# Two transformer-like blocks on one core: fewer divided matmuls, and one buffer 128 bytes further on

## The chip, the cores and the metric

One core of one Trainium2 chip runs the whole program. The metric is the device time of one execution in microseconds (us); the median over several executions is given.

## The reference

256 tokens of width 2048 go through two blocks, in float32. Cut to what matters:

```
first block:   z = rms(x) @ w_in;  differential attention and a gated spatial mix
               h = x + mixed @ w_out
               f = rms(h);  h += (silu(f @ w1) * (f @ w3)) @ w2        # hidden width 5632
               h += (p @ pl_w_up) * sigmoid(h @ pl_w_gate)             # p: per-layer input, width 256
second block:  16 meta tokens ahead of the 256
               u, gb, gc, v, ga, gbr = split(rms(h) @ w_in_2)
               y_a = pool(u) @ pool_w;  y_b = (gb * conv(gc * v)) @ conv_out_w
               h += (sigmoid(ga) * y_a + sigmoid(gbr) * y_b) @ w_o
               h += (silu(gate) * up) @ w_down                         # hidden width 5632
               out = rms(h)
```

## The kernel before, in words

Nearly all of the time is matrix products. Each weight matrix is cut into **pieces** of 256 rows by 512 columns; there are 940. SyncE's queue loads two pieces at a time (1 MB) into `raw`, a ring of four. ScalarE writes a piece's rounded high part into `hi` (L487), VectorE the rest, raw minus high, into `lo` (L814); `hi` and `lo` are rings of four pieces. The activations are held in two parts in the same way, in the buffers `A`, `B` and, for the per-layer input, `PT`.

The products are listed in order by `schedule()` as **segments**: v, qk, g, u, out, f1_up0, f1_down0, f1_up1, f1_down1, f1_up2, f1_down2, plup, plgate, ga, u2, pool, conv, gbr, cout, wo, f2_up0, f2_down0, f2_up1, f2_down1, f2_up2, f2_down2. A segment has turns, a turn has groups (two for most), and a group has pieces (8 for most, 6 in f1_down2 and f2_down2, 2 in pool, 1 in plup). A group makes 512 output columns in four banks of PSUM; its index in the turn is `g`, the piece's index in the group `j`. In the two-pass layouts a piece gives TensorE 24 matmuls of 128x128 weights by 256 columns: `highs` (L1362) makes 16, for each of two `kk` the high part of the weights with both parts of the activations (`part`), over four `m`; `lows` (L1373) makes 8, the low part of the weights with the high part of the activations. One segment follows another without a pause; the semaphores are waited for, but they are set in time.

Other forms: u2 has 272 columns and conv's first two kinds 258 columns (L1409 to L1411); v, g and the f2_down segments have 512 columns, with the activations as the stationary side (L1391 to L1393).

`turns_of` runs a segment's turns: a segment of one turn, and on TensorE the first `peel` turns of the others, are written out with `t` = 0, 1, ...; the rest is a hardware loop, in which `t` is None. f1_up0, f2_up0, out, ga and conv have `peel=1`; plup, pool and u2 have one turn; plgate, f2_up1, f2_up2, f1_down0, f1_up1 and others have `peel=0`.

`SIDE` puts small work between pieces of the first turn: in f1_up0 after piece 6 `first_ffn_rstd` (four matmuls with `ones`), in f2_up0 transposes of `h` after pieces 3 and 11 and `ffn_rstd` after piece 6, in ga `double_rstd` after piece 6.

**Divided matmuls.** In the segments that `TWO_STEPS` names, `highs` divides one matmul of the first piece (`j == 0`) of every group, the fifth of the piece, into two over neighbouring columns with the same weights: L1359 takes columns 0 to `at_col`, L1360 the rest.

**Where the buffers lie.** The tensors stand behind one another in each partition, in the order of their declarations (starts rounded up to 32 bytes). `hi` and `lo` take 16384 bytes each. From the start of `hi`, `A` begins at 35008 bytes and `B_halves`, the part of `B` that most segments read, at 69312: both 192 past a multiple of 256. `PT` stands behind `silu_s` and `UP` in an overlay and begins at 159040 bytes from `hi`, 64 past a multiple of 256. All rows within `A`, `B` and `PT`, and all weight blocks, are multiples of 256 bytes apart.

Of the kernel before, what the change touches and what calls it, by code (L numbers as in the profile page):

```python
# [23 lines left out]
F32R = mybir.dt.float32r  # L24

P = 128
D = 2048
T = 256
META = 16
TM = META + T  # L30
KT = D // P
GC = 512
MT = GC // P
# [127 lines left out]
for _step, _at in (("norm_stats", 0), ("norm_root", 1), ("norm_scale", 2)):  # L161
# [1 line left out]
SIDE.setdefault(("u", 14), []).append("gate_mix0")  # L163

TWO_STEPS = {"f1_up0": 128, "f1_down0": 240, "f1_up1": 224, "f1_down1": 192, "f1_up2": 64, "f1_down2": 16, "plgate": 252,
             "f2_up1": 248, "f2_up2": 8}

class Tally:  # L170
# [38 lines left out]
def bass_two_blocks(nc, ins, out):  # L209
    SEGS, TOTAL = schedule()  # L210

    with ExitStack() as ctx:
# [6 lines left out]
        def overlay(**shapes):  # L219

            with ExitStack() as own:
                return [own.enter_context(nc.sbuf_tensor(n, s[0], s[1])) if isinstance(s, tuple) else
                        own.enter_context(nc.sbuf_tensor(n, s, F32)) for n, s in shapes.items()]
# [13 lines left out]
        line, _, = overlay(line=[P, LINE], pad_line=[P, 1])  # L237
        _, qk = overlay(pad_qk=[P, 8 * BROW], qk=[P, 16, T])
        _, xtok = overlay(pad_x=[P, 8 * BROW], xtok=[P, 2, D])
# [18 lines left out]
        _, relb_in, meta_in, vin1, vin2, relb, onehot, lamv, rb = overlay(  # L258
            v_skip=[P, 2048 - 8], relb_in=[32, HEADS], meta_in=[META, D], vin1=[V1N, P], vin2=[V2N, P], relb=[32, HEADS, 32],
            onehot=[32, LINE], lamv=[P, 4, P], rb=[P, 2, P])  # L260
        _, ws_in = overlay(ws_skip=[P, 2 * 1024 + 2048 + 2048 + 1024 + 1024 + 1024], ws_in=[P, 8, P])
        silu_s, UP, PT = overlay(silu_s=[P, MT, T], UP=[P, KT, T], PT=([P, 2, 2 * T], F32R))
        G1, G2 = overlay(G1=[P, KT, T], G2=[P, KT, T])
        _, win_a, win_b, win_c = overlay(g1_a=[P, KT * T], win_a=[P, MT, TM], win_b=[P, MT, TM], win_c=[P, MT, TM])
        _, cvv, cvg, cvo = overlay(g1_b=[P, KT * T], cvv=[P, MT, TV], cvg=[P, MT, TV], cvo=[P, MT, T])
        _, HT, gfin_row = overlay(silu_b=[P, MT * T], HT=[P, 2, D], gfin_row=[P, D])
        sb("arena", [P, 10368])

        ps = ctx.enter_context(nc.psum_tensor("ps", [P, 8, 512], F32))
# [1031 lines left out]
        def _(pe):  # L1301
            done, v_in, s_in = Tally(pe_done), Tally(v_to_pe), Tally(s_to_pe)

            def wait(tally):
                pe.wait_ge(tally.sem, tally.now())
# [26 lines left out]
            def high(slot, kk, m):  # L1332
                return hi[:, slot % RING, kk, m * P:(m + 1) * P]
# [4 lines left out]
            def activations(buf, layout):  # L1338
                return {"A": A, "B": {"halves": B_halves, "token": B_token}.get(layout, B), "PT": PT}[buf]

            def two_passes(seg, g):

                layout = seg.reads[1]
                return layout in ("halves", "wide_halves") or (layout == "conv" and seg.kinds[g] == "cb")

            def highs(seg, g, j, slot, b0, n):

                buf, layout, _ = seg.reads
                X = activations(buf, layout)
                at = 0 if layout == "halves" else META  # L1350
                pe.wait_ge(hi_ready, n + 1)
                for kk in range(2):
                    k = 2 * j + kk + (4 * WIDEST_FIRST[g] if seg.name == "pool" else 0)
                    for part in range(2):
                        x = X[:, k, at + part * T:at + (part + 1) * T]
                        for m in range(MT):
                            at_col = TWO_STEPS.get(seg.name, 0) if j == 0 and kk == 0 and part == 1 and m == 0 else 0
                            if at_col:
                                pe.matmul(ps[:, b0 + m, 0:at_col], high(slot, kk, m), x[:, 0:at_col], start=False, stop=False)  # L1359
                                pe.matmul(ps[:, b0 + m, at_col:T], high(slot, kk, m), x[:, at_col:T], start=False, stop=False)  # L1360
                            else:
                                pe.matmul(ps[:, b0 + m, 0:T], high(slot, kk, m), x, start=j == 0 and kk == 0 and part == 0, stop=False)  # L1362

            def lows(seg, g, j, slot, b0, n):

                buf, layout, _ = seg.reads
                X = activations(buf, layout)
                pe.wait_ge(lo_ready, n + 1)
                for kk in range(2):
                    k = 2 * j + kk + (4 * WIDEST_FIRST[g] if seg.name == "pool" else 0)  # L1370
                    Xh = X[:, k, 0:T] if layout == "halves" else X[:, k, META:TM]
                    for m in range(MT):
                        last = pe.matmul(ps[:, b0 + m, 0:T], low(slot, kk, m), Xh, start=False,  # L1373
                                         stop=j == seg.pieces - 1 and kk == 1)
                last.then_inc(pieces_used, 1)
# [156 lines left out]
            def last_pieces(seg, b0):  # L1532

                first = seg.pieces - RING
                for a in range(2):
                    for j in range(first, seg.pieces):
                        n = TOTAL - seg.pieces + j
                        if a == 0:
                            pe.wait_ge(lo_ready, n + 1)
                        for kk in range(2):  # L1540
                            k = 2 * j + kk
                            Xh, Xl = B_token[:, k, a * P:(a + 1) * P], B_token[:, k, T + a * P:T + (a + 1) * P]
                            to = ps[:, b0 + a, :]
                            pe.matmul(to, Xh, hi[:, n % RING, kk, :], start=False, stop=False)  # L1544
                            pe.matmul(to, Xh, lo[:, n % RING, kk, :], start=False, stop=False)  # L1545
                            last = pe.matmul(to, Xl, hi[:, n % RING, kk, :], start=False, stop=j == seg.pieces - 1 and kk == 1)  # L1546
                        if a == 1:
                            last.then_inc(pieces_used, 1)
                    if a == 0:
                        last.then_inc(half_done, 1)  # L1550

            for seg in SEGS:
                def run(turn, t):
                    for g, kind in enumerate(seg.kinds):
                        G = turn * len(seg.kinds) + seg.g0 + g
                        b0 = 4 * ((seg.g0 + g + (t or 0) * len(seg.kinds)) % 2)
                        if seg.name == "v" and g == 1:
                            pe.wait_ge(x_kept, 2)
                        elif not isinstance(G, int) or G >= 2:
                            pe.wait_ge(psum_free, G - 1)  # L1560
                        if t == 0 and g == 0 and seg.name == "qk":
                            wait(v_in)
                            wait(s_in)
                        at_end = isinstance(G, int) and G == SEGS[-1].g0 + MT - 1
                        for j in range(seg.pieces - RING if at_end else seg.pieces):
                            n = turn * seg.per_turn + seg.p0 + g * seg.pieces + j
                            slot = seg.p0 + g * seg.pieces + j + (t or 0) * seg.per_turn
                            chunk = g if seg.name == "pool" else j // 2
                            if seg.name == "pool" and j == 0 or seg.name not in ("pool", "plup") and g == 0 and j % 2 == 0:
                                pe.wait_ge(act_ready, seg.reads[2] + chunk + 1)  # L1570
                            beside = SIDE.get((seg.name, g * seg.pieces + j), ()) if t == 0 else ()
                            if not two_passes(seg, g):
                                piece(seg, g, j, slot, b0, n)
                            else:
                                highs(seg, g, j, slot, b0, n)
                                lows(seg, g, j, slot, b0, n)
                            for what in beside:
                                side(seg, what, G)
                        if at_end:
                            last_pieces(seg, b0)  # L1580
                turns_of(pe, seg, {}, run)
# [33 lines left out]
```

## Time and profile before

| | |
|---|---|
| median of 3 runs | 2645.22 us (2645.04 to 2645.64) |
| profiled execution | 2644.93 us |
| its span, first to last instruction | 2643.1 us |
| mean granted TensorE clock | 0.999 |
| TensorE matmuls | 21427, 100% of the span busy |
| VectorE busy | 1571.9 us, 59% |
| ScalarE busy | 1172.6 us, 44% |

The profile gives each instruction of one execution its start, its duration and what released it. Matmuls overlap one another, so their durations (276 ns and more) say less than the distances between their starts. In the chain of waits a row's second number is the time up to the next link, and with equal matmuls it is that distance times their count.

### The profile page before, as it was taken

The numbers are of one execution on the slowest core, as the hardware profiler recorded it, in microseconds if no ns is written. First come the engines' busy times: TensorE is split into PE (matmuls) and PEld (weight loads), VectorE is DVE, ScalarE is ACT, GpSimd is POOL, SyncE is SP. The second block draws the span as 40 slices with busy tenths as digits, with TensorE's granted clock in tenths as the row PEclk, the third lists the DMA queues.
The fourth block names the chain that finished last, engine by engine and source line by source line (L and its number), as shares of the span: only waits on it lengthen the run. The fifth ranks groups of instructions, "written<-read, shape, count | busy, mean of one in ns | idle before, by whom it ended". The sixth has DMA issues, their size and how long they took to land.

```text
span 2643.1 us, 50947 instructions
## 1 busy us (share of the span) xinstructions
PE 2630.4 (100%) x21427; PEld 2568.2 (97%) x21427; DVE 1571.9 (59%) x1557; ACT 1172.6 (44%) x1259; POOL 0.8 (0%) x7
## 2 busy tenths in 40 slices
PE   9999999999999999999999999999999999999998
PEld 7989999999999999999999999999999989998997
DVE  6567765555555556795666666556755555554555
ACT  5446544434443444454433333444554434443444
POOL 0000000000000000000000000000000000000000
PEclk9999999999999999999999999999999999999999
DMA  8644655555655565555555555655555555555553
GB/s 295 197 162 148 204 192 191 191 192 190 194 188 199 189 199 192 177 203 194 176 176 190 179 189 178 201 189 198 191 194 195 199 192 191 190 191 191 190 191 128
DMA packets 254275, 503.33 MB, mean 190 GB/s; under 512 B 8130, under 2 KB 11652, under 8 KB 253988
## 3 DMA queue, kind: packets, MB, share of 16 engines
q1 hardware_dynamic: 252180, 497.61, 56.8%
q10 hardware_dynamic: 1952, 3.68, 0.4%
q8 instruction: 106, 1.74, 0.3%
q14 instruction: 37, 0.30, 0.0%
HBM read 498.37 MB, written 2.88 MB: 190 GB/s over the span
## 4 chain that ended last, share of the span: by engine, by line
PE 99%; DMA 0%; DVE 0%; ACT 0%; SPq 0%; issue 0%; DVEq 0%; ACTq 0%
PE ps L1362 49%; PE ps L1373 24%; PE ps L1391 4%; PE ps L1393 4%; PE ps L1392 4%; PE ps L1409 4%; PE ps L1410 4%; PE ps L1411 4%; PE ps L1401 0%; PE ps L1402 0%; PE ps L1403 0%; DMA xtok<-in_x_dram 0%; PE ps L1360 0%; PE ps L1546 0%; PE ps L1545 0%; PE ps L1544 0%
## 5 line engine op out<-in xcount | busy, mean ns | idle before, releaser
L814 DVE TENSOR_TENSOR lo<-raw,hi 128x1024 fp32r<-128x1024 f32 x940 | 1144.2, 1224 | 931.3 <-ACT hi L487 916.8
L487 ACT ACTIVATE hi<-raw 128x1024 fp32r<-128x1024 f32 x940 | 991.3, 1060 | 1255.8 <-PE ps L1373 945.9
L1362 PE MATMUL ps<-A,hi 128*128 128x256 f32 x7256 | 909.1, 277 | 0.0
L1362 PEld LDWEIGHTS ps<-A,hi 128*128 128x128 f32 x7256 | 863.3, 188 | 0.3
L1362 PE MATMUL ps<-B,hi 128*128 128x256 f32 x3956 | 491.6, 276 | 0.0
L1373 PE MATMUL ps<-A,lo 128*128 128x256 f32 x3648 | 489.3, 277 | 0.0
L1362 PEld LDWEIGHTS ps<-B,hi 128*128 128x128 f32 x3956 | 468.0, 188 | 0.1
L1373 PEld LDWEIGHTS ps<-A,lo 128*128 128x128 f32 x3648 | 448.8, 188 | 0.0
L1373 PE MATMUL ps<-B,lo 128*128 128x256 f32 x1984 | 265.2, 276 | 0.0
L1373 PEld LDWEIGHTS ps<-B,lo 128*128 128x128 f32 x1984 | 243.3, 188 | 0.0
L1410 PE MATMUL ps<-B,hi 128*128 128x258 f32 (+1 forms) x768 | 219.7, 286 | 0.0
L1411 PE MATMUL ps<-B,lo 128*128 128x258 f32 (+1 forms) x768 | 219.5, 286 | 0.0
L1409 PE MATMUL ps<-B,hi 128*128 128x258 f32 (+1 forms) x768 | 219.4, 286 | 0.0
L1409 PEld LDWEIGHTS ps<-B,hi 128*128 128x128 f32 x768 | 145.9, 190 | 0.0
L1411 PEld LDWEIGHTS ps<-B,lo 128*128 128x128 f32 x768 | 145.4, 189 | 0.0
L1410 PEld LDWEIGHTS ps<-B,hi 128*128 128x128 f32 x768 | 144.2, 188 | 0.0
L1392 PE MATMUL ps<-lo,B 128*128 128x512 f32 x336 | 130.7, 389 | 0.0
L1393 PE MATMUL ps<-hi,B 128*128 128x512 f32 x336 | 130.7, 389 | 0.0
L1391 PE MATMUL ps<-hi,B 128*128 128x512 f32 x336 | 130.7, 389 | 0.0
L1393 PEld LDWEIGHTS ps<-hi,B 128*128 128x128 f32 x336 | 63.1, 188 | 13.1
L1391 PEld LDWEIGHTS ps<-hi,B 128*128 128x128 f32 x336 | 63.1, 188 | 13.0
L1392 PEld LDWEIGHTS ps<-lo,B 128*128 128x128 f32 x336 | 63.1, 188 | 13.0
(247 smaller groups left out, 1226.7 us busy)
## 6 DMA issues: line engine op xcount, KB each, us to landing
raw<-in_w_in_dram SPq DMA_DIRECT2D x136, 1024.0 KB, 5.1
raw<-in_ffn_w_dram SPq DMA_DIRECT2D x132, 1024.0 KB, 5.1
raw<-in_w_gate_up_dram SPq DMA_DIRECT2D x88, 1024.0 KB, 5.0
raw<-in_w_down_dram SPq DMA_DIRECT2D x44, 1024.0 KB, 5.0
raw<-in_w_out_dram SPq DMA_DIRECT2D x16, 1024.0 KB, 4.9
raw<-in_pl_w_gate_dram SPq DMA_DIRECT2D x16, 1024.0 KB, 5.0
raw<-in_conv_out_w_dram SPq DMA_DIRECT2D x16, 1024.0 KB, 5.0
raw<-in_w_o_dram SPq DMA_DIRECT2D x16, 1024.0 KB, 5.0
```

The lines of the kernel that those rows point to most:

```text
L487: act.activation(hi[:, slot % RING], raw[:, raw_slot, 2 * (slot % 2):2 * (slot % 2) + 2, :], ACT.Copy).then_inc(hi_ready, 1)
L814: dve.tensor_tensor(lo[:, slot % RING], raw[:, slot // 2 % RAWS, 2 * (slot % 2):2 * (slot % 2) + 2, :], hi[:, slot % RING], ALU.subtract). ...
L1362: pe.matmul(ps[:, b0 + m, 0:T], high(slot, kk, m), x, start=j == 0 and kk == 0 and part == 0, stop=False)
L1373: last = pe.matmul(ps[:, b0 + m, 0:T], low(slot, kk, m), Xh, start=False, stop=j == seg.pieces - 1 and kk == 1)
L1391: pe.matmul(to, Xh, hi[:, slot % RING, kk, :], start=first, stop=False)
L1392: pe.matmul(to, Xh, lo[:, slot % RING, kk, :], start=False, stop=False)
L1393: last = pe.matmul(to, Xl, hi[:, slot % RING, kk, :], start=False, stop=final)
L1409: pe.matmul(to, Wh, Xh, start=first, stop=False, skip_group_check=True)
L1410: pe.matmul(to_low, Wh, Xl, start=False, stop=False, skip_group_check=True)
L1411: last = pe.matmul(to, Wl, Xh, start=False, stop=final, skip_group_check=True)
```

## The change

`TWO_STEPS`, with a column for each of nine segments and every group, gives way to one column, 248, and a list of places. A place is a segment's name with the index of a piece in the turn (`g * seg.pieces + j`). In the turn with `t == 0` the list `IN_STEPS` holds, in every other turn the shorter list `IN_STEPS_EVER`. The divided matmul is still the fifth of its piece. The products are the same. `PT` gets 32 float32 words (128 bytes) ahead of it in its overlay.

```diff
-TWO_STEPS = {"f1_up0": 128, "f1_down0": 240, "f1_up1": 224, "f1_down1": 192, "f1_up2": 64, "f1_down2": 16, "plgate": 252,
-             "f2_up1": 248, "f2_up2": 8}
+STEP = 248
+IN_STEPS_EVER = {("f2_up1", 0), ("f2_up2", 0)}
+IN_STEPS = IN_STEPS_EVER | {("f1_up0", 8), ("plup", 0), ("plgate", 0), ("pool", 0), ("f2_up0", 8), ("f2_up0", 12)}
...
-        silu_s, UP, PT = overlay(silu_s=[P, MT, T], UP=[P, KT, T], PT=([P, 2, 2 * T], F32R))
+        silu_s, UP, _, PT = overlay(silu_s=[P, MT, T], UP=[P, KT, T], pad_pt=[P, 32], PT=([P, 2, 2 * T], F32R))
...
-            def highs(seg, g, j, slot, b0, n):
+            def highs(seg, g, j, slot, b0, n, in_steps):
...
-                            at_col = TWO_STEPS.get(seg.name, 0) if j == 0 and kk == 0 and part == 1 and m == 0 else 0
-                            if at_col:
-                                pe.matmul(ps[:, b0 + m, 0:at_col], high(slot, kk, m), x[:, 0:at_col], start=False, stop=False)
-                                pe.matmul(ps[:, b0 + m, at_col:T], high(slot, kk, m), x[:, at_col:T], start=False, stop=False)
+                            if in_steps and kk == 0 and part == 1 and m == 0:
+                                for a, b in ((0, STEP), (STEP, T)):
+                                    pe.matmul(ps[:, b0 + m, a:b], high(slot, kk, m), x[:, a:b], start=False, stop=False)
...
-                                highs(seg, g, j, slot, b0, n)
+                                highs(seg, g, j, slot, b0, n, (seg.name, g * seg.pieces + j) in (IN_STEPS if t == 0 else IN_STEPS_EVER))
```

## Rows read from the trace of the kernel before

**Rows 1.** The page: span, TensorE's granted clock in 40 slices, the last chain.
```profile
span 2643.1 us, 50947 instructions
...
PEclk9999999999999999999999999999999999999999
...
PE 99%; DMA 0%; DVE 0%; ACT 0%; SPq 0%; issue 0%; DVEq 0%; ACTq 0%
```

**Rows 2.** The page's groups: the work on each piece beside TensorE's.
```profile
L814 DVE TENSOR_TENSOR lo<-raw,hi 128x1024 fp32r<-128x1024 f32 x940 | 1144.2, 1224 | 931.3 <-ACT hi L487 916.8
L487 ACT ACTIVATE hi<-raw 128x1024 fp32r<-128x1024 f32 x940 | 991.3, 1060 | 1255.8 <-PE ps L1373 945.9
```

**Rows 3.** Line L1359, the first part of every divided matmul.
```profile
L1359 PE MATMUL ps<-A,hi x40: 168/242/277, 343.9 to 2547.4; 128*128 128x128 f32 x8, 128*128 128x224 f32 x8, 128*128 128x248 f32 x8, 128*128 128x64 f32 x6
...
L1359 PE MATMUL ps<-B,hi x12: 172/248/269, 519.8 to 1050.5; 128*128 128x240 f32 x4, 128*128 128x192 f32 x4, 128*128 128x16 f32 x4
```

**Rows 4.** Chain of waits (start, us, what): gbr's first piece, f2_up0's first.
```profile
1646.33 1.81 PE ps L1362 x16
...
1907.45 1.81 PE ps L1362 x16
```

**Rows 5.** Chain: divided matmuls of f1_up0 (turns 1 to 3), f1_up1, f1_down2: first and last.
```profile
388.63 0.06 PE ps L1359
...
498.06 0.06 PE ps L1359
...
607.44 0.10 PE ps L1359
...
760.55 0.10 PE ps L1359
...
1001.29 0.01 PE ps L1359
...
1050.62 0.01 PE ps L1359
```

**Rows 6.** Chain: end of f1_down2, plup's first piece, plgate's first matmuls.
```profile
1065.69 0.91 PE ps L1373 x8
1066.60 1.88 PE ps L1362 x16
...
1077.91 0.46 PE ps L1362 x4
```

**Rows 7.** Chain: pool's first matmuls, and conv's first.
```profile
1350.60 1.89 PE ps L1362 x16
...
1373.21 0.12 PE ps L1409
```

**Rows 8.** Chain: f1_up0, the piece behind `first_ffn_rstd`, and piece 8's second part.
```profile
363.45 1.89 PE ps L1362 x16
...
368.23 0.91 PE ps L1373 x8
```

**Rows 9.** Chain: f2_up0 from `ffn_rstd` on, the transposes, piece 12.
```profile
1928.69 1.88 PE ps L1362 x16
...
1942.83 1.75 PE ps L1495 x16
1944.58 1.83 PE ps L1362 x16
1946.41 0.91 PE ps L1373 x8
```

**Rows 10.** Chain: f2_up1's first piece, divided into 248 and 8.
```profile
2173.09 0.47 PE ps L1362 x4
...
2175.05 0.91 PE ps L1373 x8
```

**Rows 11.** Chain: f2_up2, its first three groups' divided pieces, and its end.
```profile
2435.17 0.47 PE ps L1362 x4
...
2457.89 0.47 PE ps L1362 x4
...
2459.85 0.91 PE ps L1373 x8
...
2481.77 0.94 PE ps L1373 x8
...
2568.89 0.94 PE ps L1373 x8
2569.83 0.23 PE ps L1391
```

## The prediction

> **What bounds the kernel now.** I read the page first: the chain that ended last is 99% TensorE, at a granted clock of nine tenths or more in every slice, which with the mean of 0.999 given in the table is the 2.4 GHz level throughout [rows 1]. So whatever changes TensorE's own stream changes the time one for one. VectorE and ScalarE need 1.22 and 1.06 us for each piece of weights [rows 2]; a piece takes TensorE 2.72 us [rows 4], and the waits of both engines before these instructions are long and end mostly on each other or on TensorE. A stream faster by some thousandths does not run into them, nor into the transfers of 1 MB for two pieces.
>
> Next I read the chain of waits piece by piece. A piece of 24 matmuls of 256 columns (16 with `hi`, 8 with `lo`) has one of two cadences. The reader should compare the durations of the "x16" and "x8" rows: 1.81 and 0.91 us, or 1.88 and 0.94.
> - **Plain:** gbr, cout and wo, 96 pieces or 2304 matmuls with no split and no interruption, take 1907.45 - 1646.33 = 261.12 us, 113.33 ns each [rows 4]. The three segments run in loops, and cross from B to A, to B and to A.
> - **Stretched:** pool takes (1373.21 - 1350.60) / 192 = 117.8 ns each [rows 7]; plup, (1077.91 - 1066.60) / 96 = 117.8 [rows 6]. It is 4.43 ns more for each matmul, at the same clock. Once there, f2_up2 stays there until something interrupts the run of equal matmuls [rows 11].
>
> **What a split costs in the plain cadence.** The 24 matmuls take 25 starts. From one divided matmul to the next lie 192 plain intervals (21.76 us) and what the split adds: with 128 and 128 columns (498.06 - 388.63) / 5 = 21.89 us, so 0.13; with 224 and 32 (760.55 - 607.44) / 7 = 21.87, so 0.11; with 16 and 240, over 144 intervals (16.32), (1050.62 - 1001.29) / 3 = 16.44, so 0.12 [rows 5]. That is 0.11 to 0.13 us a split, about one whole matmul interval, however few columns the smaller part has. I take 0.13 where the smaller part has 64 columns or more, 0.12 in f1_down2 and 0.11 elsewhere; the range over all 41 removed here is 4.5 to 5.3 us. 
>
> **The change, part by part.**
> 1. *Splits removed in plain stretches.* Before there are 40 + 12 = 52 [rows 3]. After, by the code: `t == 0` exists for the engine only where a segment has one turn or a first turn peeled off. f1_up0 keeps one (its piece 8), f2_up1 four and f2_up2 three, one a turn; plup, pool get one, f2_up0 two. plgate has two turns and nothing peeled on TensorE, so its `t` is None and its entry does nothing. That makes 12. Removed outside f2_up2: f1_up0 7 x 0.13, f1_down0 4 x 0.11, f1_up1 8 x 0.11, f1_down1 4 x 0.13, f1_up2 6 x 0.13, f1_down2 4 x 0.12, plgate 4 x 0.11, f2_up1 4 x 0.11 = 4.89 us. None of it lies beside other work on TensorE's path. That the plain cadence needs no upkeep is what rows 4 show; without that the price is that of rival 1.
> 2. *f2_up2.* It takes 2569.83 - 2435.17 = 134.66 us [rows 11], against 1152 x 113.33 = 130.56: 4.10 over. Its turns begin stretched, or are put there: the 8 and 248 split leaves one group stretched (2435.17 to 2457.89), the next plain (2459.85), the third stretched again (2481.77). f2_up1 is entered from the same kind of 512-column matmuls, also stretched (0.47 for four), and its 248 and 8 split brings it to plain at 2175.05 [rows 10], for 1.96 - 1.81 = 0.15 us. f2_up2 is now split in that way. New excess: 0.15 + 2 x 0.11 = 0.37. Gain 3.73 us. Bounds: 4.10 at most; if the split failed, all 1152 stretched (5.10) and three splits, a loss of 1.3.
> 3. *pool.* Now 192 x 4.43 ns = 0.85 over. With the split at the same place as in f2_up1 it should cost 0.15: gain 0.70. Bounds: -0.11 to 0.74.
> 4. *f2_up0.* After the norm's matmuls five pieces are stretched, 1928.69 to 1942.83 [rows 9]. The split in piece 8 leaves 28 stretched matmuls and ends the other 92 early: 92 x 4.43 = 0.41, less 0.13 for the split made in a stretched stream (0.15 less four stretched matmuls). The transposes after piece 11 restore the plain cadence already before the change (0.91 at 1946.41), so the split of piece 12 buys nothing and costs 0.11. Gain 0.17; bounds -0.24 to 0.30.
> 5. *f1_up0's piece 8* stays split, 248 and 8 instead of 128 and 128. It is entered stretched and must be left plain, as it is now [rows 8]. I count 0 for the other size, with 0.02 either way.
> 6. *PT 128 bytes on.* Entering plup the cadence changes with the first matmul that reads PT, and after it recovers within four matmuls on A (0.46 at 1077.91, before the next split) [rows 6]. By the declared sizes A and B_halves begin 192 bytes past a multiple of 256 from `hi`, PT 64; moved by 128, PT is as they are. I expect plain: 0.43 saved, 0.11 for the new split, 0.32 net. Bounds -0.11 to 0.32. No wait is added anywhere, no DMA or queue is touched, and UP and PT still fit into the arena.
>
> Sum: 4.89 + 3.73 + 0.70 + 0.17 + 0.32 = 9.81 us off the profiled execution's 2644.93 (span 2643.1 and 1.8 around it): 2635.1. The median of the runs is 0.3 above that execution, so 2635.4.
>
> **Rivals.**
> 1. *The stretched cadence is not left in f1_up0* (slower). What ends it there now is a split of 128 and 128; 248 and 8 has one witness from a stretched stream [rows 10], none in this place, and the same two parts in the other order fail in one entry and work in another [rows 11]. Nothing behind it interrupts the stream up to plup: 256 pieces, 6144 matmuls x 4.43 = 27.2 us. With plup's split as rescue: 2635.4 + 27.2 = 2662.6; without, 1032 more up to ga's norm, 2667. If the change from A to B at f1_down0 healed it (PT to A healed plup's), 56 pieces, 6.0 us: 2641.4. It decides from 9.81 / 0.00443 = 2200 matmuls, 92 pieces. For it: no safeguard is left. Against: 248 and 8 left a stretched stream plain, and 128 and 128 did here. 0.16, of which healed 0.03. A plain stream that falls stretched unaided in the same region would cost the same kind of sum; rows 4 speak against it.
> 2. *f2_up2's first split fails:* 1.3 lost instead of 3.73 won, 2640.5. Against it stands the like entry of f2_up1. 0.05.
> 3. *The small places fail* (pool, f2_up0, one or both): 0.8 + 0.4 at most, 2636.6. 0.08.
> 4. *The address does nothing:* plup stays at 117.8 and pays for a split: 0.32 + 0.11, 2635.9. That would be so if TensorE's reads met no obstacle that depends on the place; against it, both changes of cadence in rows 6 come with the buffer. 0.07. The Trainium skill (SBUF — State Buffer, Who interferes with whom) gives PE two independent read ports and says that it never waits on anyone, which is this rival; rows 6 do not agree with it easily.
>
> **How the numbers follow.** The summed forecast has 0.64. Within 2634.5 (all splits at 0.13) and 2641 lie forecast, rivals 2, 3 and 4: 0.84. A no-change reading is 0.2%, 5.3 us, either way. Faster: 0.64 + 0.08 + 0.07 = 0.79. Same: rival 2 and the healed part of rival 1, 0.08. Slower: 0.13.
>
> **What the profile after would show.** 12 split pairs; "x16" rows of 1.81 us from f1_up0's piece 9 on through f1_down2, without a break; PT rows of 1.81; in pool 1.88 for nothing past its first few matmuls; f2_up2 about 130.9 us long; f2_up0's pieces 9 to 11 at 1.81. If 1.88 stands behind 366 us, rival 1 is true and the prediction wrong; rows of 1.88 only from 2435 us on mean rival 2.

## The result, and the profile after

2668.52 us, median of four executions (2668.50 to 2668.55), against 2645.22: ratio 1.0088, 95% interval 1.007 to 1.0105. 23.3 us slower, where 9.8 us faster was forecast. The profiled execution took 2668.52 us with a span of 2666.7.

The page of the changed kernel: the span, the granted clock in 40 slices, the last chain. Only the span differs in a way that matters.

```profile
span 2666.7 us, 50867 instructions
...
PEclk9999999999999999999999999999999999999999
...
PE 99%; DVE 1%; ACT 0%; DMA 0%; issue 0%; DVEq 0%; ACTq 0%
```

TensorE is still the whole chain, at the full 2.4 GHz level (nine tenths or more in every slice; the mean granted clock is 0.999). The loss is a cadence, that is, the time from one matmul's start to the next one's, and the chain of waits of the changed kernel shows it (start, us, what; a divided matmul is now one row, L1360 x2). First f1_up0 from the norm's matmuls on, then plup's first piece and the last two pieces before ga's norm.

```profile
363.67 1.89 PE ps L1362 x16
...
366.50 0.47 PE ps L1362 x4
366.97 0.12 PE ps L1360 x2
...
368.49 0.94 PE ps L1373 x8
369.43 1.89 PE ps L1362 x16
...
1090.70 0.12 PE ps L1360 x2
...
1092.22 0.94 PE ps L1373 x8
...
1210.94 0.94 PE ps L1373 x8
1211.89 0.86 PE ps L1487 x4
...
1214.58 0.91 PE ps L1373 x8
```

The reader should follow the "x8" rows. Before, the piece behind the division had 0.91 [rows 8]; now it has 0.94, and so has every one up to ga's norm: 1211.89 - 366.50 = 845.39 us for 299 pieces, 7176 matmuls, 117.8 ns each. The division did not end the stretched cadence in f1_up0, and the one in plup did not either. ga's norm ended it.

Two other places failed too. In the chain, pool's first piece and f2_up0's piece 8 keep 0.94 behind their divisions (first two rows), whereas f2_up2's first piece goes to 0.91 (fourth row), as f2_up1's did before [rows 10] and does here; the last row is f2_down2's start:

```profile
1380.03 0.94 PE ps L1373 x8
...
1961.06 0.94 PE ps L1373 x8
...
2462.48 0.47 PE ps L1362 x4
...
2464.45 0.91 PE ps L1373 x8
...
2593.42 0.23 PE ps L1391
```

f2_up2 took 2593.42 - 2462.48 = 130.94 us instead of 134.66: the 3.7 us that were forecast there did come. The same two parts work in f2_up1 and f2_up2 and fail in the four others (f1_up0, plup, pool, f2_up0's piece 8). What differs is in the rows of the weight loads. In a stretched run their durations repeat 188, 188, 192 ns (a 188 is at times a 187); in a plain run all have 187 or 188. The next rows are the groups by line of the changed kernel, each in a window that only one load touches: the last two loads ahead of the divided matmul's own, in f1_up0 (around 366.55 and 366.67 us), then in f2_up1 (around 2200.91 and 2201.03).

```profile
L1362 PEld LDWEIGHTS ps<-A,hi 128*128 128x128 f32 x1 | 0.2, 188 | 0.0
L1362 PEld LDWEIGHTS ps<-A,hi 128*128 128x128 f32 x1 | 0.2, 192 | 0.0
...
L1362 PEld LDWEIGHTS ps<-A,hi 128*128 128x128 f32 x1 | 0.2, 192 | 0.0
L1362 PEld LDWEIGHTS ps<-A,hi 128*128 128x128 f32 x1 | 0.2, 188 | 0.0
```

Call a division **place 1** when the load directly ahead of its own is the 192, **place 2** when the load before that one is, **place 3** otherwise. f1_up0, plup, pool and f2_up0's piece 8 are divided at place 1, f2_up1 and f2_up2 at place 2. The kernel before holds such a pair for 8 and 248 columns, with the places the other way round: divided at place 2 in f2_up2's first group (first two rows, around 2435.22 and 2435.34 us), which stayed stretched, and at place 1 in its second (last two, around 2457.95 and 2458.07), which left the stretched cadence [rows 11].

```profile
L1362 PEld LDWEIGHTS ps<-A,hi 128*128 128x128 f32 x1 | 0.2, 192 | 0.0
L1362 PEld LDWEIGHTS ps<-A,hi 128*128 128x128 f32 x1 | 0.2, 188 | 0.0
...
L1362 PEld LDWEIGHTS ps<-A,hi 128*128 128x128 f32 x1 | 0.2, 188 | 0.0
L1362 PEld LDWEIGHTS ps<-A,hi 128*128 128x128 f32 x1 | 0.2, 192 | 0.0
```

### The profile page after: what moved, and what is told of

Read it like the earlier page. It is cut to its first block, busy times and chain, and to the rows that moved or that the text cites. A ratio compares the mean times of both kernels' runs of the same rounds, so it can differ in the third digit from the quotient of the medians.

```text
span 2666.7 us, 50867 instructions
## 1 busy us (share of the span) xinstructions
PE 2655.4 (100%) x21387; PEld 2593.1 (97%) x21387; DVE 1572.6 (59%) x1557; ACT 1172.2 (44%) x1259; POOL 0.8 (0%) x7
## 4 chain that ended last, share of the span: by engine, by line
PE 99%; DVE 1%; ACT 0%; DMA 0%; issue 0%; DVEq 0%; ACTq 0%
PE ps L1362 49%; PE ps L1373 24%; PE ps L1391 4%; PE ps L1393 4%; PE ps L1392 4%; PE ps L1409 4%; PE ps L1410 4%; PE ps L1411 4%; PE ps L1401 0%; PE ps L1403 0%; PE ps L1402 0%; DVE lo L815 0%; PE ps L1319 0%; DMA xtok<-in_x_dram 0%; PE ps L1546 0%; PE ps L1545 0%
## 5 line engine op out<-in xcount | busy, mean ns | idle before, releaser
L1362 PE MATMUL ps<-A,hi 128*128 128x256 f32 x7285 | 918.3, 279 | 0.0
L1362 PEld LDWEIGHTS ps<-A,hi 128*128 128x128 f32 x7285 | 876.0, 188 | 0.3
L1362 PE MATMUL ps<-B,hi 128*128 128x256 f32 x3968 | 497.2, 278 | 0.0
L1373 PE MATMUL ps<-A,lo 128*128 128x256 f32 x3648 | 495.3, 278 | 0.0
```

## The experiments

The code below is cut to what each run changes. Theory A: the place in the cycle of three, together with the two parts, decides whether a division ends a stretched run. The rivals: the removed divisions had kept the plain cadence up (B); the parts alone, or what ran before, decide (C).

**1. 128 and 128 again, in f1_up0 alone.**

```diff
-for a, b in ((0, STEP), (STEP, T)):
+for a, b in ((0, in_steps), (in_steps, T)):        # 128 for ("f1_up0", 8), else 248
```

> The changed kernel with one edit: the divided matmul of f1_up0's piece 8 is 128 and 128 columns again, all other places as changed. Theory A (the loss is the stretched cadence, 117.8 ns a matmul, carried from f1_up0's piece 8 to ga's norm because 248 and 8 does not end it there): 6144 + 96 + 768 + 168 matmuls x 4.44 ns = 31.9 us come back, 2668.5 becomes 2636.6; pool (117.8) and f2_up0's pieces 8 to 11 stay stretched. Theory B (the removed divisions kept the plain cadence up, so it would be lost again in one of the loops): most of the 23 us stays, 2650 to 2668, and the 1.88 rows begin again somewhere between 390 and 1090 us.

Measured: 2636.50 us (median of six), ratio to the kernel before 0.9967 (0.9953 to 0.9981). One number of one matmul carries 32 us. The chain:

```profile
366.23 0.47 PE ps L1362 x4
366.70 0.17 PE ps L1360 x2
...
368.18 0.91 PE ps L1373 x8
369.09 1.81 PE ps L1362 x16
...
1062.68 0.45 PE ps L1362 x4
...
1064.61 0.91 PE ps L1373 x8
...
1179.76 0.86 PE ps L1487 x4
```

From 366.23 to ga's norm it is 813.53 us, against 845.39 in the changed kernel: 31.86, as theory A said, to 0.1 us. Theory B falls: 41 divisions are gone from plain stretches, and the plain cadence holds through all the loops: all 297 "x16" rows behind piece 8 up to ga's norm are 1.81.

**2 and 3. The same two parts, one and two matmuls later**, in f1_up0's piece 8, pool's first piece and f2_up0's piece 8:

```diff
-if in_steps and kk == 0 and part == 1 and m == 0:
+if in_steps and kk == 0 and part == 1 and m == in_steps - 1:     # 2 (then 3) in f1_up0, pool and f2_up0's piece 8
```

> The changed kernel with the same 248 and 8 columns, but in f1_up0's piece 8, pool's piece 0 and f2_up0's piece 8 the sixth matmul of the piece is divided instead of the fifth. In a stretched run the weight loads show a cycle of three (188, 188, 192 ns); where 248 and 8 failed, the matmul right behind a 192 was divided, where it worked (f2_up1, f2_up2), the second behind. Theory A (the place in that cycle decides): all three places go plain, 2668.5 - 31.9 - 0.8 (pool) - 0.4 (f2_up0) = 2635.4. Theory C (the size or what ran before decides, not the place): nothing changes, 2668.5.

> As the run before, but the seventh matmul of the piece is divided, the third behind a 192 in the cycle. Theory A has no witness for this place; that all three places behave alike is what it says: either all three leave the stretched cadence (about 2635.4) or none (2668.5). Theory C: none, or a mixture.

Measured: 2640.85 us (ratio 0.9984, 0.9972 to 0.9995) and, in one execution, 2640.79. In both, all three went plain: f1_up0's piece 9 at 1.81, pool 21.9 us instead of 22.7, f2_up0's pieces 9 to 11 at 1.81. That is theory A, and C is out: the parts and what ran before are the changed kernel's. But the time expected was 2635.4: 5.5 us were missing, and the chain of the run at the sixth matmul shows where, in f2_up0 from the transposes on:

```profile
1936.50 0.91 PE ps L1373 x8
1937.41 1.75 PE ps L1495 x16
1939.16 0.47 PE ps L1362 x4
1939.63 0.12 PE ps L1360 x2
...
1941.15 0.94 PE ps L1373 x8
```

The transposes are now entered plain (0.91 ahead of them), and behind the division in piece 12 the stream is stretched up to f2_down0: the rest of piece 12 and 51 pieces more, 5.5 us.

**4. Without the division in piece 12:**

```diff
-... ("pool", 0), ("f2_up0", 8), ("f2_up0", 12)}
+... ("pool", 0): (2, 248), ("f2_up0", 8): (2, 248)}     # (m, columns); f1_up0 as well; piece 12 is out
```

> The run that divides the seventh matmul in f1_up0's piece 8, pool's piece 0 and f2_up0's piece 8, now without the division in f2_up0's piece 12 (and without the idle entry for plgate). Theory D: the transposes after piece 11 leave a stream that settles to plain by itself in some four matmuls, as those after piece 3 do, and the division in piece 12 falls into those matmuls and turns it stretched for the 52 pieces up to f2_down0 (5.1 us); without it f2_up0 is plain from piece 12 on and the time is 2640.8 - 5.1 - 0.1 - 0.3 = 2635.3. Theory E: the transposes leave it stretched when they are entered plain, and the division merely fails to help: the time stays 2640.7.

Measured: 2635.34 us (ratio 0.9962, 0.9948 to 0.9976), as theory D said. The chain of the same place:

```profile
1937.40 1.75 PE ps L1494 x16
1939.14 1.84 PE ps L1361 x16
1940.98 0.91 PE ps L1372 x8
```

Behind the transposes the stream settles to plain by itself; the division, in the fifth matmul, caught it before it had. The same division costs only 0.1 us in the changed kernel, where the transposes are entered stretched. The starts in the traces show the difference: there the stream has settled sooner, and the last two distances ahead of the division are 113 and 113 ns. In run 2 they are 117 and 119, and in run 4, without the division, the first 113 stands between the seventh and the eighth matmul.

**5. One division for each entry**, none in plain stretches: f2_up1 and f2_up2 with `peel=1` and divided in turn 0 only, plup undivided; five in all.

> As the run before, and the divisions in plain stretches are gone too: f2_up1 and f2_up2 have their first turn written out and are divided there alone (3 + 2 fewer), plup is not divided. Five divisions in all. If a plain stream needs no upkeep and a division costs 0.11 us: 0.68 us less than the run before, 2634.6. If it needs upkeep, 1.88 rows appear in f2_up1 or f2_up2, up to 5 us more.

Measured: 2635.14 us (2634.76 to 2635.41), ratio 0.9961 (0.9947 to 0.9974). The span is 0.7 us below that of run 4 (2632.9 and 2633.6, in the profile and as the medians of the five executions of each), as six intervals of 0.11 us should make it. The medians of the whole time differ by 0.2 us only and their ranges overlap: the time outside the span was longer here, so the gain is read from the spans alone.

**6 and 7. Other parts at other places.**

```diff
-IN_STEPS of run 4: ("f1_up0", 8): (2, 248), ("pool", 0): (2, 248), ("f2_up0", 8): (2, 248)
+run 6:             ("f1_up0", 8): (0, 8),   ("pool", 0): (1, 8),   ("f2_up0", 8): (2, 8)
+run 7:             ("f1_up0", 8): (1, 128), ("pool", 0): (2, 128), ("f2_up0", 8): (1, 128)
```

> Parts in the other order, 8 and 248, at three places of the cycle of three: right behind the 192 ns weight load in f1_up0's piece 8, second behind in pool, third behind in f2_up0's piece 8; no division in piece 12. Theory A (place and parts together decide; in the kernel before, 8 and 248 left the stretched cadence right behind a 192 and not at the second place): f1_up0 plain, pool stretched (0.8 us more than with 248 and 8 there), f2_up0 unknown: 2636.1 to 2636.6. If the order of the parts alone decided, f1_up0 would stay stretched, as f2_up2's first group did: 2667.

> 128 and 128 columns at the second place behind the 192 in f1_up0's piece 8 and f2_up0's piece 8, and at the third in pool; no division in piece 12. Right behind a 192 this division works. Theory A has no witness for the two other places; if equal parts work at any place, 2635.4; if the second place fails, f1_up0's stretched cadence runs to ga's norm, 2667.

Measured, one execution each: 2636.21 and 2635.30 us. In run 6 f1_up0 and f2_up0 went plain and pool alone did not, as the kernel before had foretold for place 2. Pool's first piece in the chain of run 6:

```profile
1346.21 0.59 PE ps L1361 x5
1346.80 0.23 PE ps L1359 x2
...
1348.20 0.94 PE ps L1372 x8
```

All divisions in a stretched run but those behind the transposes, with the activations at a start 192 bytes past a multiple of 256 from `hi`, of both kernels and of the runs up to here:

| parts | place 1 | place 2 | place 3 |
|---|---|---|---|
| 248 and 8 | stays (f1_up0, plup, pool, f2_up0) | leaves (f2_up1, f2_up2, run 2) | leaves (runs 3, 4, 5) |
| 8 and 248 | leaves (f2_up2 before, run 6) | stays (f2_up2 before, run 6) | leaves (run 6) |
| 128 and 128 | leaves (before, run 1) | leaves (run 7) | leaves (run 7) |

Three limits of the table:
- The index of the divided matmul in its piece does not explain it. Before, f2_up2 divided the fifth matmul of every group; its fourth and fifth groups were both entered stretched, and divided at place 2 and at place 1. The one stayed stretched, the other left:

```profile
2504.49 0.94 PE ps L1373 x8
...
2527.19 0.91 PE ps L1373 x8
```

- It does not hold for a stream that is still settling. Behind the transposes in runs 2 and 3 the loads ahead of the division are 192, 188, 188 too (place 3), and behind 248 and 8 the stream was stretched.
- It says nothing of plain runs, and there a division can do harm: 8 and 248 turned f2_up2's third and sixth groups stretched in the kernel before, though each was entered plain (0.91 at 2459.85, 0.94 at 2481.77 for the third [rows 11]). None of the other parts did so in a plain run.

**8. No division in f1_up0**, the changed kernel otherwise (`("f1_up0", 8)` out of the list).

> The changed kernel without the division in f1_up0's piece 8. If 248 and 8 did nothing there but take one interval: 0.11 us less than the changed kernel, 2668.4, with the same stretched pieces from 366 us on. If the stream behind the norm's matmuls would settle by itself and the division keeps it stretched: about 2636.5.

Measured, one execution: 2668.82 us; the span is 2667.0. f1_up0 itself is 180.82 us long instead of 180.92, the one interval. The program's start took 0.4 us longer in this execution, which hides it in the total. A stretched run does not settle by itself, and the division there did nothing.

**9. The start of PT, and of A.** Run 1 without `pad_pt`; run 5 with `pad_pt=[P, 16]` and `[P, 48]` instead of 32; and run 5 with `rstd_meta` (64 bytes) declared behind A, which moves A 64 bytes back. Besides A only `tiny` and `rstd_meta` itself move, two small tensors that no long run of matmuls reads.

> As the first run (128 and 128 in f1_up0's piece 8), but PT lies where it lay before, without the 128 bytes. If the address of PT makes plup's cadence: plup at 117.8 ns entered from a plain stream, recovered within plgate's first matmuls, 0.4 us more than the first run, and plup at 113.3 in the first run. If the address does nothing, plup has the same cadence in both and the times agree to 0.1 us in the span.

> The five-division kernel with PT 64 bytes further on than before the change instead of 128 (128 past a multiple of 256 from hi; 64 before the change, 192 with it). If the place modulo 256 bytes makes the cadence, plup is either 10.88 us long (113.3 ns) or about 11.3 (117.8) and recovers in plgate; no witness for which. If the address does nothing, 10.88. The rest unchanged, 2634.6 to 2635.5.

> The same with PT 192 bytes further on, at a multiple of 256 from hi. Again 10.88 or about 11.3 us for plup.

> The five-division kernel with rstd_meta (64 bytes) declared behind A instead of ahead of it, so that A alone begins 64 bytes earlier, 128 past a multiple of 256 from hi; B, PT and the rest stay. If the place modulo 256 decides and not the buffer, A's plain pieces take the cadence that PT has in the run with PT at 128: 113.3 ns and 2635, or 117.8 ns on about 11000 matmuls, some 48 us more, with B's segments at 113.3. If a different place merely changes how entries settle, single segments change.

Measured, one execution each: 2637.47, 2636.19, 2635.95 and 2702.89 us. plup, entered plain each time, in the chain: with PT as before the change (divided, first three rows), then 64 bytes on.

```profile
1063.33 0.47 PE ps L1362 x4
...
1065.32 0.94 PE ps L1373 x8
1066.26 1.88 PE ps L1362 x16
...
1074.74 1.82 PE ps L1362 x16
```
```profile
1063.18 1.90 PE ps L1361 x16
1065.08 0.95 PE ps L1372 x8
...
1074.57 1.82 PE ps L1361 x16
```

Each has plgate's first piece as its last row. By distance from `hi` modulo 256 bytes plup's 96 matmuls take 117.7 ns at 64 (11.41 us less a division's 0.11), 118.6 at 128, 119.8 at 0 (11.50 us), and 113.3 at 192, where the change puts it (10.88 us in run 5). The 10.88 or 11.3 us that were expected for 128 and for 0 came in neither. With A at 128, qk's first and last pieces and the start of g:

```profile
61.33 1.90 PE ps L1361 x16
...
149.62 1.90 PE ps L1361 x16
151.52 0.95 PE ps L1372 x8
152.47 0.23 PE ps L1390
```

(152.47 - 61.33) / 768 = 118.7 ns, the figure of PT at 128. qk, f1_up1, plgate and cout, all on A, took it, and gbr, on B at 192, kept 1.81. f1_down0 and f1_down1, on B but entered from such a stream, ran at 117.8, f1_down2 at 113.3: a start at 192 does not always end what came before. The start decides and not the buffer; 64 bytes cost 67.8 us on 2635.1. Expected were 48, with all of B's segments plain: the matmuls on A cost 5.3 ns more each and not 4.4, and f1_down0 and f1_down1 add 6.8 us. Behind each of this run's five divisions A's cadence was 118.7. The runs moved the activations and never the weights, so they do not tell whether the distance from the weights counts or the address by itself.

## Why the prediction was wrong

**The step that failed** is part 5, f1_up0's piece 8, "I count 0 for the other size": 248 and 8 at place 1 keeps a stretched run stretched. It was worth 31.9 us (run 1), and it turned -9.8 into +23.3. Rival 1 named the mechanism, the place and its end at ga's norm, and gave 2667 for a failure in plup too (about 2668 with the gains of pool and f2_up0's piece 8 lost as well); it had 0.16. The one witness from which I took the opposite, f2_up1, was at another place in the cycle. The sign that this mattered stood in the trace of before: 8 and 248 failing in one group and working in the next. I wrote it down and did not ask what differed between the two; the weight loads ahead of them did.

**Point by point.**
- *What bounds:* right. 7176 matmuls at 4.44 ns more are 31.9 us in the time.
- *Divisions removed, 4.89 us:* right. In run 1 f1_down0 is 87.04 us long instead of 87.49 and f1_up1 174.08 instead of 174.99; the plain cadence needs no upkeep.
- *f2_up2, 3.73:* measured 3.72, in the changed kernel itself.
- *pool, 0.70, and f2_up0, 0.17:* wrong for the same reason as part 5; 0.11 and 0.22 lost. Runs 2 and 3 show pool's gain when the division is at place 2 or 3.
- *f2_up0's piece 12, "buys nothing and costs 0.11":* right for the changed kernel (0.11), where the transposes are entered stretched. Had piece 8 worked as I assumed, it would have cost 5.5 us (runs 2 and 3), and the forecast would have been 2640.9. This trap was not in the sum.
- *PT, 0.32:* right in mechanism, but it showed only in run 1 (plup 10.99 us instead of 11.31). In the changed kernel plup was entered stretched. Rival 4 falls: at the four starts that were tried plup has four cadences. The Trainium skill (SBUF — State Buffer, Who interferes with whom) gives PE two independent read ports and says that it never waits on anyone. That does not cover this: the runs of experiment 9 show TensorE's cadence depend on where its moving operand lies.
- *Entry for plgate does nothing:* right.

Account of the spans, 2643.1 to 2666.7: f1_up0 to ga +27.1 (31.9 stretched, less the divisions gone there), pool +0.1, f2_up0 +0.2, f2_up1 -0.45, f2_up2 -3.7, the start of the program +0.3; together 23.6.

What stays open is why the place in the cycle of three and the parts decide as the table has it. The runs give the table and no mechanism below it.

## What to carry to other kernels

A stream of equal matmuls can have more than one stable cadence at the same clock, and an interruption chooses one that then lasts until the next: look at the distance between starts, piece by piece, before looking for waits. A remedy that depends on the phase must be witnessed at its own place, or be one that works at every place (here 128 and 128 columns, at all three); before safeguards are removed, count what a failure of the last one costs. A division is not harmless either: 8 and 248 turned a plain stream stretched. Look at the start of the moving operand modulo 256 bytes: in this kernel 64 bytes were worth 67.8 us.

## What the runs showed of the hardware

- 256-column matmuls, each with a load of its own weights, came every 113.33 ns or every 117.8, at a granted clock of 0.999 both times; a stretched run of 7176 matmuls did not recover (run 8, without a division up to plup), and a plain one as long did not decay (run 1, with one division in it; run 5, with none behind f1_up0's piece 8).
- The weight loads of a stretched run repeat 188, 188, 192 ns, and that phase, with the two parts, goes with what a divided matmul does in such a run (table). In a plain run 8 and 248 started the stretched cadence; a division of other parts cost 0.11 to 0.13 us and started nothing.
- The cadence depends on the moving operand's start. By its distance from the weights, which stayed where they were, modulo 256 bytes: 113.3 ns at 192 (A, B, PT), 118.6 at 128 (PT, A), 117.7 at 64 and 119.8 at 0 (PT alone). On A, 64 bytes made 67.8 us.
- Behind sixteen transposes of 128 columns the stream settles to plain by itself, whether they are entered stretched (0.91 at 1946.41 [rows 9]) or plain (0.91 at 1940.98, run 4). Entered plain, it settles later, and a division in the fifth matmul behind them made it stretched (runs 2 and 3).
